# Modulation chunks moved into the first projection, decays made ahead of their loop, and other places for taps, halves, scaling and the context's norm

## The reference

```
# block 1
mod   = silu(c) @ w_ada + b_ada                  # 6 x 1024; the same for c_ctx
h     = rmsnorm(x) * (1 + mod[1]) + mod[0]
gq, gk, gv, gz, gg, rq, rk, rv, rg = split(h @ w_in)      # 3616 columns
gate  = log_sigmoid(gz @ gla_gate_w + b) / 16    # the decays of the gated linear attention
o_g   = head_rmsnorm(gla(gq,gk,gv,gate) both directions) * silu(gg)
o_r   = head_layernorm(retention(rq,rk,rv,log_gamma) both directions) * silu(rg)
x     = x + mod[2] * (concat(o_g, o_r) @ w_out)
h2    = rmsnorm(x) * (1 + mod[4]) + mod[3]
x     = x + mod[5] * expert_choice_ffn(h2)       # 16 experts, each takes its 32 best tokens
x     = rmsnorm(x) * final_norm_w
# block 2, twice (layer l = 0, 1), with its own modulation mod = silu(c) @ ada_w[l] + ada_b[l]
z     = modulate(rms_norm(x)) @ w_in[l]          # 10 parts of 256
y_a   = silu(layer_norm(depthwise_conv(a_val * sigmoid(a_gate), 31 taps)))
y_b   = differential attention(q, k, v of x and context), 4 heads, rms_norm per head
y_c   = gelu(u) * (w_s @ layer_norm(gelu(sv)) + b_s)      # spatial gating
y_d   = bg * depthwise_conv(cg * xin, 3 taps)
x     = x + mod * (concat(y_a, y_b, y_c, y_d) @ w_out[l])
x     = x + mod * (square(relu(modulate(rms_norm(x)) @ w1)) @ w2)
# the context gives layer l only keys and values, from its own norm and modulation
out   = rms_norm(x) * final_g
```

## Time and profile before

| what | value |
|---|---|
| median of three runs | 1956.15 us (1955.53 to 1956.22) |
| the profiled execution's own time | 1952.86 us |
| its span in the trace | 1951.0 us |
| PE busy | 1739.5 us, 89% of the span |
| DVE, ACT, POOL busy | 878.2, 553.9, 134.1 us |
| moved by DMA | 526.59 MB, mean 270 GB/s |

### The profile page before, as it was taken

How to read it: one execution, slowest core, us unless ns; L and a number is a source line. 1 busy time by engine, 2 the same in 40 slices (tenths; PEclk the granted TensorE clock), 3 DMA queues, 4 the chain that set the end, 5 groups by cost and what they waited for, 6 DMA issues and landing times.

```text
span 1951.0 us, 30618 instructions
## 1 busy us (share of the span) xinstructions
PE 1739.5 (89%) x13078; PEld 1309.2 (67%) x13078; DVE 878.2 (45%) x1550; ACT 553.9 (28%) x955; POOL 134.1 (7%) x145
## 2 busy tenths in 40 slices
PE   4999997889998899889989998968999989689997
PEld 1699765555554555555555556846999969479997
DVE  3223433223453211211112126865677777867775
ACT  3124321230230110000000004335544453454443
POOL 0000000100000000000000003400000013000000
PEclk8899988989999999999999998979999999699999
DMA  7224773769999999999999994745354413134530
GB/s 308 95 87 152 318 285 144 302 267 426 424 425 423 425 424 425 425 425 425 424 425 424 425 425 199 308 189 194 142 198 179 172 67 145 49 130 149 196 130 22
DMA packets 60165, 526.59 MB, mean 270 GB/s; under 512 B 6410, under 2 KB 9738, under 8 KB 22160
## 3 DMA queue, kind: packets, MB, share of 16 engines
q1 hardware_dynamic: 45888, 471.18, 59.5%
q0 software_dynamic: 14160, 53.70, 6.9%
HBM read 523.80 MB, written 1.05 MB: 269 GB/s over the span
## 4 chain that ended last, share of the span: by engine, by line
PE 58%; DMA 29%; DVE 8%; ACT 3%; POOL 1%; issue 1%; SPq 0%; DVEq 0%; ACTq 0%
PE bank L801 58%; DMA big<-in_w_exp_down 13%; DMA big<-in_w_exp_up 8%; DMA big<-in_w_exp_gate 4%; DVE big L2002 2%; DVE big L2536 1%; DMA big<-in_ada_half 1%; DMA big<-in_w_ada 1%; DMA big<-in_ada_w 1%; DVE big L2039 1%; DVE big L2025 1%; DVE w_lo L2002 1%; DVE h_lo L2032 1%; POOL big L784 0%; DVE big L2669 0%
## 5 line engine op out<-in xcount | busy, mean ns | idle before, releaser
L801 PE MATMUL bank<-big 128*32 128x352 f32 (+8 forms) x7454 | 1025.9, 427 | 162.3 <-DMA big<-in_w_exp_down 32.8
L801 PEld LDWEIGHTS bank<-big 128*32 128x32 f32 (+4 forms) x7454 | 616.3, 147 | 556.6 <-issue 300.4
L801 PE MATMUL bank<-h_lo,w_hi 128*128 128x256 f32 (+1 forms) x1568 | 450.6, 287 | 0.0
L801 PE MATMUL bank<-h_hi,w_hi 128*128 128x256 f32 x1408 | 404.5, 287 | 34.6 <-DVE h_lo L2032 22.5
L801 PE MATMUL bank<-h_hi,w_lo 128*128 128x256 f32 x1408 | 402.9, 286 | 0.0
L801 PEld LDWEIGHTS bank<-h_lo,w_hi 128*128 128x128 f32 x1568 | 305.3, 195 | 0.7
L801 PEld LDWEIGHTS bank<-h_hi,w_hi 128*128 128x128 f32 x1408 | 273.2, 194 | 45.0 <-issue 29.3
L2002 DVE TENSOR_TENSOR w_lo<-big,w_hi 128x1024 fp32r<-128x1024 f32 x188 | 234.0, 1253 | 145.0 <-ACT w_hi L1975 59.4
L801 PEld LDWEIGHTS bank<-h_hi,w_lo 128*128 128x128 f32 x1408 | 271.0, 192 | 0.7
L2002 DVE TENSOR_TENSOR big<-big 128x256 f32<-128x256 f32 (+6 forms) x199 | 107.2, 544 | 216.2 <-ACT big L1837 147.2
L1975 ACT ACTIVATE w_hi<-big 128x1024 fp32r<-128x1024 f32 x120 | 126.5, 1054 | 97.3 <-PE bank L801 97.3
(11 more groups left out here) (241 smaller groups left out, 1221.0 us busy)
## 6 DMA issues: line engine op xcount, KB each, us to landing
big<-in_w_exp_gate SPq DMA_DIRECT2D x64, 1408.0 KB, 21.9
big<-in_w_exp_up SPq DMA_DIRECT2D x64, 1408.0 KB, 22.1
big<-in_w_exp_down SPq DMA_DIRECT2D x48, 1536.0 KB, 22.8
big<-in_mlp_w SPq DMA_DIRECT2D x32, 2048.0 KB, 7.9
big<-in_w_in SPq DMA_DIRECT2D x17, 2048.0 KB, 8.8
big<-in_u_w POOLq DMA_DIRECT2D x64, 512.0 KB, 9.2
big<-in_w_ada SPq DMA_DIRECT2D x12, 2048.0 KB, 12.5
big<-in_ada_w SPq DMA_DIRECT2D x12, 2048.0 KB, 11.5
```

The lines of the kernel that those rows point to most:

```text
L801: return nc.tensor.matmul(o, l, r, start=start, stop=stop)
```

## The change

It changes places, buffers and widths; what is computed stays.

- Start: the norm's sums come before chunks 0 and 1 on PE, the reciprocal before the modulation on DVE, the square root before the copies of chunks on ACT, and the first two weight splits before the norm's.
- First projection: chunks 4 to 12 are made between its pairs (`PROJ1_ADA`), in buffers that lie where results of the mixer go later, in banks 4 and 5. The gate products move into pair 4, in banks 6 and 5. The logarithms are made one pair earlier, `modulation(12, ...)` at pair 6.
- Mixer of block 1: chunks 13 to 21 in place of 4 to 17; a head's decays are made by ACT and DVE between the GLA steps (`retention_decay`), all q decays in a row before the loop; the loop keeps the multiplications of q and of the scores. Squares of the GLA half are made earlier.
- After it: chunks 22 and 23 in place of 18 to 23, loaded before the expert weights.
- Block 2, layer 0: a third buffer for the halves; halves 0 and 1 after the norm's sums, 2 to 11 in the projection, 12 and 13 after it, 10 in attention. POOL's scaling of x after unit 19. Seven taps of the convolution move from before attention into attention's units 0 to 2 (in layer 1 they go to earlier units of the projection). The statistics of sv (sum, square, square root) are made by ACT. The tail of the mixer has another order.
- Context's norm for layer 1: squares on ACT in the output projection of layer 0, sums on PE after its norm sums, scaling and splitting in the last MLP round; so layer 1's first norm is T wide.
- The last norm and the store go in four pieces of two k tiles.

```diff
+        ADA = [(0, 0, "slot1", 0), (0, 2, "slot2", 1), (0, 1, "own0", 2), (0, 3, "own1", 0)]
+        ADA += [(0, 4 + n, ("own2", "own1")[n % 2], 4 + n % 2) for n in range(7)]
+        ADA += [(0, 11, "own1", 5), (1, 0, "own1", 4)]
+        ADA += [(1, 1 + n, f"slot{(1, 0, 2)[n % 3]}", n % 3) for n in range(9)]
+        ADA += [(1, 10 + n, ("late0", "late1")[n], n) for n in range(2)]
+        ADA_FIRST, ADA_MIX, ADA_LATE = 4, 13, 22
+        PROJ1_ADA = {0: (4,), 1: (6,), 2: (7, 8), 3: (9, 10), 4: (11,), 5: (12,)}
...
 # SP
+            for i in range(2, 5):
+                ada_load(i)
+            w_in_load(1)
+            ada_own(5)
+            ada_own(6)
+            w_in_load(2)
...
             sp.wait_ge(S("mix1_ready"), 1)
-            ada_load(18)
-            ada_load(19)
-            sp.wait_ge(S("ada_ps"), 19)
-            ada_load(20)
+            ada_load(22)
+            ada_load(23)
...
-                if n in (2, 4, 5):
-                    late = {2: 21, 4: 22, 5: 23}[n]
-                    sp.wait_ge(S("ada_ps"), late - 1)
-                    ada_load(late)
...
+            for q in range(4):
+                sp.wait_ge(S("final"), 2 * q + 2)
+                sp.dma_start(out[:, 2 * q:2 * q + 2, :], resid[:, 2 * q:2 * q + 2, 0:T]).then_inc(S("stored"), 16)
...
 # POOL
-                    if n == 0 and layer == 0:
+                    if j == 19 and layer == 0:
                         pool.wait_ge(S("r1_ready"), 1)
...
 # PE
+            norm_sums(0, N2)
             for i in range(2):
                 ada_step(i)
             ada_columns()
-            norm_sums(0, N2)
...
+                    if p == 1 and x == 1:
+                        ada_step(5)
+                    if p == 4 and x == 0:
+                        pe.wait_ge(*tiles.emptied(q))
+                        pe.wait_ge(S("ada_part"), 10)
+                        for tt_ in range(4):
+                            if tt_ >= 2:
+                                pe.wait_ge(S("gate_out"), tt_ - 1)
+                            m = mm(PB[(6, 5)[tt_ % 2]], gz[0:33, tt_ * P:(tt_ + 1) * P], gw[0:33, :])
+                            m.then_inc(S("gate_ps"), 1)
...
+                if p in PROJ1_ADA:
+                    if p == 4:
+                        pe.wait_ge(S("gate_out"), 4)
+                    ada_step(*PROJ1_ADA[p])
...
+                    for k in range(KT):
+                        pe.wait_ge(S("cx_sq"), k + 1)
+                        m = mm(PB[5][:, 0:T], ones, h[:, k, T:N2], k == 0, k == KT - 1)
+                    m.then_inc(S("ss"), 1)
...
 # ACT
+            def decays(hh):
+                if hh >= 2:
+                    act.wait_ge(S("dec_ready"), hh - 1)
+                for d in range(2):
+                    i_ = A(dec_t[:, hh % 2, d * 512:(d + 1) * 512], c1("rel", 2, 512)[:, d, :], ACT.Exp,
+                           scale=lg[:, 0, d * 4 + hh:d * 4 + hh + 1])
+                i_.then_inc(S("dec_in"), 1)
...
+                link(A(s4[:, 10:12], s4[:, 8:10], ACT.Copy, scale=-1.0 / GW))
+                for m_ in range(2):
+                    i_ = A(sv_dev[:, m_, :], sv[:, m_, :], ACT.Square, bias=s4[:, 10 + m_:11 + m_],
+                           accum_out=s4[:, 12 + m_:13 + m_])
+                link(i_)
+                A(s4[:, 12:14], s4[:, 12:14], ACT.Sqrt, bias=eps_t, scale=1.0 / GW).then_inc(S("sv_std"), 1)
...
 # DVE
+            def retention_decay(hh):
+                dve.wait_ge(S("dec_in"), hh + 1)
+                b = hh % 2
+                link(tt(dec_t[:, b, :], dec_t[:, b, :], c1("msk", 1024), ALU.mult))
+                tt(dec[hh], dec_t[:, b, 0:512], dec_t[:, b, 512:1024], ALU.add).then_inc(S("dec_ready"), 1)
...
-                        conv_a(24, 27)
...
+                    if u < 3 and layer == 0:
+                        conv_a(24 + 3 * u, 27 + 3 * u)
...
+                        if last and layer == 0 and n < 9:
+                            if n:
+                                context_low(n - 1)
+                            if n < 8:
+                                V.scalar_tensor_tensor(h[:, n, T:N2], resid[:, n, T:N2], asc[:, 4, n, 1:2], rs[:, T:N2],
+                                                       ALU.mult, ALU.mult).then_inc(S("cx_scaled"), 1)
```

More of the change, by code:

```diff
@@ L1065, in _, with head_squares @@
                 ret_values(hh)
-            ada_step(16)
-            def head_squares(first):
+            def head_squares(first, squares):
                 for hh in range(4):
@@ L1542, in mlp_pe @@
                                         m.then_inc(S(f"h1_ps{c}"), 1)
+                    if layer == 0 and paired:
+                        pe.wait_ge(S("mod_out"), 7)
+                        pe.wait_ge(S("rms"), 7)
                     for c in range(2):
@@ L1674, in _ @@
             i_.then_inc(S("decay_out"), 1)
+            decays(1)
             act.wait_ge(S("gla_step"), 4)
@@ L1938, in _ @@
                         h_high(MIX_ORDER[:2])
+                act.wait_ge(S("pv_ps"), u0 + len(units))
+                A(tc, PB[6][:, :].rearrange("p (a b) -> p a b", a=2), ACT.Square).then_inc(S("osq_ready"), 1)
+                act.wait_ge(S("yc_ready"), layer + 1)
+                h_high(MIX_ORDER[2:4])
+                act.wait_ge(S("oss_ps"), layer + 2)
+                A(rs, PB[4], ACT.Sqrt, bias=eps_t, scale=1.0 / 64).then_inc(S("o_rms"), 1)
                 act.wait_ge(S("ln_out"), layer + 2)
@@ L1975, in mlp_round @@
                             A(round_split(w_hi, m), w_unit(m), ACT.Copy).then_inc(S("w_hi_ready"), 1)
+                        if n < 8 and last and layer == 0:
+                            act.wait_ge(S("cx_scaled"), n + 1)
+                            A(h_hi[n][:, T:N2], h[:, n, T:N2], ACT.Identity, bias=modv[:, 2, n, 1:2]).then_inc(S("cx_hi"), 1)
                         if n >= 12 and last:
-                            nx = N2 if layer == 0 else T
+                            nx = T
                             for dt in (2 * q, 2 * q + 1):
@@ L2053, in modulation @@
                     tt(modv[:, layer, first:last, :],
-                       PB[bank][:, 96 * layer + 2 * first:96 * layer + 2 * last].rearrange("p (a b) -> p a b", b=2),
+                       PB[bank][:, 2 * first:2 * last].rearrange("p (a b) -> p a b", b=2),
                        bc(v0("bada", 3, 48)[:, layer, first:last], 2, [P, last - first, 2]), ALU.add) \
@@ L2696, in _ @@
                 norm_rest(k0 + 1, nf)
+                if layer == 0:
+                    dve.wait_ge(S("rms"), 7)
+                    V.reciprocal(rs[:, T:N2], rs[:, T:N2])
+                    dve.wait_ge(S("ada2_cols"), 24)
+                    tt(modv[:, 2, :, :], PB[7][:, 256:352].rearrange("p (a b) -> p a b", b=2),
+                       bc(v0("bada", 3, 48)[:, 2, :], 2, [P, 48, 2]), ALU.add).then_inc(S("mod_out"), 1)
+                    dve.wait_ge(S("mod_out"), 7)
+                    scales(4, 5)
                 def take_unit(i, n):
```

379 lines of the change are left out of this document (203 added, 176 removed), and 4 rows, old and new, of the table sgw.

## The result

| what | before | changed |
|---|---|---|
| median | 1955.84 us (4 runs, 1938.73 to 1956.22) | 1879.36 us (4 runs, 1878.24 to 1880.69) |
| ratio (of the means of the runs) | 1 | 0.963, 95% interval 0.9577 to 0.9683 |
| profiled execution | 1952.86 us, span 1951.0 | 1880.31 us, span 1878.5 |
| mean granted clock | 0.945 | 0.962 |

A forecast was written before the change was run, and what follows sets the result against it. The prediction took the limit stage by stage: PE alone in the first projection, memory transfer in the experts, PE's waits elsewhere. Its terms summed to -56.0 us, from 1956.15 to 1900, with eight of ten in 1877 to 1926.

The forecast's parts named there:

- The start's order: Start: norm's sums ahead of chunks 0 and 1 move the first product from 52.7 to about 43; -9.8 us.
- the late chunks: Output projection and router: four chunks and two load waits leave, only 22 and 23 (and columns of 21) stay; -20.5 us.
- the gap before layer 0's attention: Block 2, layer 0: taps and statistics leave DVE, ACT's own chain is then last; -3 us, wait 8 to 9, not 11.6.
- Rival C: First projection: chunk matmuls pull following products to half clock; over all of it net +57 us, 2013; chance 0.05.
- Rival B: First projection: chunk loads arrive late, +14 us, 1914, or 1925 with other terms low; chance 0.08.
- the mixer: Block 1's mixer: five chunks, a load wait, decays and tail give -24.6 us, 5.6 taken back for uncovered waits; -19.
- the clock: PE's granted clock in single stages: +1.5 us added in the first projection, -2.2 in router, -1 in layer 1's attention.
- Case D: Removed fillers give their whole time; clock in mixer, out projection and attention rises to 0.94; -75.6 us, 1880; chance 0.17.
- The scaling's move: Block 2, layer 0: scaling of x leaves the place where PE waited for POOL's w_lo; -2.7 us, new place nothing net.
- The taps': Layer 0: tap operations leave DVE before attention and go into units 0 to 2, costing 3.3 us there; stage -14.
- Case E: Before attention, POOL's scaling locks the port shared with DVE for all 13.8 us; 1905, at most 1909; chance 0.05.
- The store: End of kernel: store in four pieces, the last of 256 KB, the others under the norm; -2.1 us (0 to -3.6).

The follow-up runs named there:

- e5: Changed kernel with half of the row matmuls (8 of 16) of chunks 4 to 12 left out in the first projection; median 1877.87 us.
- e4: Changed kernel with the decays made in the retention loop again, as before the change, chunks where the change puts them; 1890.04 us.
- e2: Kernel before with only the change's block 2 part, block 1 as before; 1914.05 us, ratio 0.9827 to the kernel before.
- e12: As e11, with the added matmuls fitted to the waits, more waits filled, and e10's load order; 1867.35 us, ratio 0.9573 to the kernel before.
- e6: Changed kernel with half of the row matmuls of chunks 13 to 21 left out, mostly in block 1's mixer; 1887.87 us.
- e3: The whole changed kernel, run again beside the kernel before on the same chip; 1880.98 us, ratio 0.964.
- e8: Changed kernel with POOL's scaling of x back after the first unit of layer 0; median 1878.58 us.
- e9: Changed kernel with the seven last taps of layer 0's convolution before attention again; median 1881.45 us.
- e10: Changed kernel with half chunks 14 and 15 put ahead of the second MLP load on the load queue; median 1878.45 us.
- e11: Changed kernel with 120 constant 128x128 matmuls, results unread, added where PE waits in block 1's mixer and around layer 1's attention; 1884.89 us.

## Why the prediction was right, and where it was off

*Right, by its own steps.* Nothing but PE bounds the first projection, and it takes nine chunks at their price (e5). The start's order, the late chunks, the widths of layer 1's norm, and the chain before layer 1's attention came within 2 us of their terms; the decays' part came at 6.8 for 6 (e4), and the gap before layer 0's attention shrank by the 3.0 of its term (the wait that the prediction named as its sign, 8 to 9, is 3.25, as two half chunks stand in that gap). The experts shifted whole. Rival C (the clock of the projection) has its counter in the stage's clock, 0.96, above the 0.94 of before, and in e5. Rival B falls: there is no wait for a load in the projection.

*The term that was mis-sized* is the mixer: "where one is gone, part of the wait it covered comes up ... I take 5.6 back". Next to nothing was to be taken back: -24.7 against the sum of -24.6 without it (or -22.7, with e2's 115.0 as the stage before). Waits on DVE fell, 15.9 to 11.8, by the decays (e4). The five chunks weren't put back singly; their part is what e4 leaves. In the router the step did hold once: with chunk 20 gone from in front of it, PE's wait for ACT grew from 0.9 to 3.5. That stage still met its -20.5, with its clock at 0.94 in place of 0.86.

The second is the clock, which stood in the sum as -1 to -2.2 in places and as +1.5 in the projection. Mean clock went from 0.945 to 0.962. The half-speed time by the spans, 215 us before and 143 after, is worth 14 us at e12's 0.2 for each and up to 31 at 0.43 (estimates), some of which the sum had. It fits what is over the forecast in the projection (+21.7 for +25, where the forecast had added 1.5 and the clock rose from 0.94 to 0.96) and may have a part in attention of layer 1 (-3.5 for -1, 0.83 to 0.88); how much it has of each stage wasn't tested singly. The experts' -2.8 isn't the clock's: DMA is used 1.00 there, and e2 has 770.5 with block 1 as before.

*Case D has the number, but only half of its reason.* The 5.6 were had; its clock was not: it put mixer, output projection and attention at 0.94, and they came to 0.89, 0.94 and 0.84 (layer 0) or 0.88 (layer 1). About 4 us of its number are the lag between profiled execution and median, and the projection gave 3.3 that D didn't name.

*Right for a poor reason.* The counter to case D was that fillers cover waits. e6 shows that the fillers do matter, and that with half of what is left the mixer is 6.7 longer; five whole ones could go since PE, in e3's trace, has no wait of over a us until 278.8. So the outcome was close to an edge that the prediction didn't see: it priced a filler by its own length and the wait behind it, and not by the clock that may go with it.

*Priced, but not seen in the time.* The scaling's move (-2.7 in the sum) brought nothing (e8). The taps' in layer 0 (part of the -14) brought 1.8 in the trace and nothing that a median can tell (e9). The statistics on ACT and the order of halves and tail weren't undone singly and stay open between them.

*Case E, the port.* Beside POOL's first operation seven taps took 3.7 in place of 2.8 and two products 1.6 in place of 1.4; beside the second two products took 5.7 in place of 1.4. So some 5.3 of the 13.3 us were lost on DVE, about the 5 taken, and well under what the Trainium skill's exclusive lock ("SBUF — State Buffer", section "SBUF: two separate sides") would give over both. The trace disagrees with the lock for the first operation, where seven taps went on, and agrees for the second, where one product took 4.99. It agrees too for POOL's weight split ahead of them, beside which one tap took 2.59. ACT's chain hid it: the wait before attention ended with ACT.

*Its bounds.* The single bounds of the prediction add to about -80 and -18, not to -79 and -23; the range was set apart from them, and nothing hangs on it.

*The store* landed in 2.2 a piece and the last norm to the end took 2.5 less; the stage's +0.4 is MLP time, whose clock was 0.96 in place of 0.97, 4.6 us more at half level.

## What to carry over

Price a filler in an order of work twice: by its own time, and by the wait that it would leave open; then look at the clock behind its place, since the mixer got longer, not shorter, when half of each of its chunks was left out (e6). Where a queue has waits that can't be closed, constant matmuls of just their length were worth 11 us here (e12 against e10), and ones half again too long cost 4 (e11). Move independent work to the stage where its engine is the only limit and the other resources idle: it cost there about its own length (21.7 us for nine chunks priced at 23.7). And when a wait shrinks, measure the gap from the last piece of the stage's own work, since a filler put into a wait shortens the wait and not the time.

## What the runs showed of the hardware that was not expected

- A wait of PE of 1.56 us, in a mixer with half of its chunk matmuls, was followed by a clock of 0.58 over 32 us (e6); about the same steps without the wait and with all of the chunk matmuls had 0.87. In e3 a wait of 1.41 us was followed by 1.00, and the clock fell to the half level at 260 us with no wait at all: the length of a wait doesn't tell it.
- Waits of 2.7 to 3.1 us in the tail of block 1's mixer filled with matmuls brought the router stage behind, whose work is the same, from 0.94 to 1.00 and from 54.2 to 51.1 us (e12).
- 36 runs of the kernel before spread over 1.3% (1938.7 to 1963.7), with the clock from 0.955 to 0.942 in those that list it; eight of the changed kernel over 0.3% (1877.6 to 1883.1) at 0.959 to 0.965, and six with filled waits over 0.35% at 0.971 to 0.978.
- A float32 matmul of 128x128 on 128x128 took 0.23 us at full clock (4.2 us for 18, 11.0 for 48) and counts as two instructions in the trace (18 gave 36).
- A DVE multiply-add of 128x256 took 2.59 us beside POOL's tensor_tensor, ending 0.3 after it, and 0.52 each beside POOL's tensor_scalar, in place of 0.41.
